# In-projection tiles in four parts, with the background steps between them

## What is computed

```python
proj = h @ w_in                       # 1024 -> 4608 columns
rq, rk, rv, rg, dq, dk, dv = jnp.split(proj, EVEN_SPLITS, axis=-1)
rq = rope(rq.reshape(B, L, H_RET, DK_RET), pos)
rk = rope(rk.reshape(B, L, H_RET, DK_RET), pos)
ro, s_fin = retention(rq, rk, rv.reshape(B, L, H_RET, DV_RET), s0)
ro = head_group_norm(ro).reshape(B, L, RET_V) * jax.nn.silu(rg.astype(F32))
dq = rope(rms_norm(dq.reshape(B, L, 2 * H_DIFF, DH_DIFF), qg), pos)
dk = rope(rms_norm(dk.reshape(B, L, 2 * H_DIFF, DH_DIFF), kg), pos)
k_all = jnp.concatenate([k_past, dk], axis=1)     # samples: 32 pages of 128 positions each
do = diff_attn(dq, k_all, v_all, pos, k_pos, lam)
mix = jnp.concatenate([ro, do], axis=-1) @ w_out
```

## Time and profile before

| | us |
|---|---|
| median of 3 runs | 2005.0 (2004.58 to 2010.87) |
| profiled execution | 2001.99 |
| its span | 2000.2 |
| TensorE busy | 1858.2 (93%) |
| VectorE, GpSimd, ScalarE busy | 897.7, 648.7, 603.4 |
| mean granted TensorE clock | 0.961 |

### The profile page before, as it was taken

The page is one execution under the profiler, slowest core; times in us unless marked ns, Lnnn a source line. Parts: engine busy times, 40 slices in busy tenths (PEclk is TensorE's granted clock), DMA queues, the critical chain, the costliest instruction groups (busy, mean ns, idle before and its releaser), DMA issues.

```text
span 2000.2 us, 31022 instructions
## 1 busy us (share of the span) xinstructions
PE 1858.2 (93%) x12203; PEld 1498.2 (75%) x12203; DVE 897.7 (45%) x1230; ACT 603.4 (30%) x986; POOL 648.7 (32%) x482
## 2 busy tenths in 40 slices
PE   4968888798889999999999999999999999999998
PEld 3866656566567777777778887767668799999997
DVE  3676554554667765543243325432223453223321
ACT  5323335433223231122233332131322332212311
POOL 0674323343456998634111000130221334103400
PEclk8888889899889999999999999999999999999999
DMA  7244534676878888865355565868783233323231
GB/s 251 91 143 127 169 127 158 198 253 224 293 263 274 267 286 295 304 190 176 125 170 147 190 201 177 284 207 284 254 281 106 86 95 94 95 88 93 84 103 57
DMA packets 296722, 365.43 MB, mean 183 GB/s; under 512 B 15625, under 2 KB 228186, under 8 KB 296330
## 3 DMA queue, kind: packets, MB, share of 16 engines
q1 hardware_dynamic: 289354, 355.36, 54.7%
q10 hardware_dynamic: 6640, 6.95, 1.0%
q0 software_dynamic: 592, 1.25, 0.5%
HBM read 352.29 MB, written 11.21 MB: 182 GB/s over the span
## 4 chain that ended last, share of the span: by engine, by line
PE 61%; issue 25%; DVE 5%; ACT 4%; POOL 3%; DMA 1%; SPq 1%; ACTq 0%; DVEq 0%; POOLq 0%
PE ps L2222 8%; PE ps L2224 8%; PE ps L2223 8%; PE ps L2309 6%; PE ps L2311 6%; PE ps L2310 6%; PE ps L2011 3%; PE ps L1945 3%; PE ps L1946 3%; PE ps L1947 3%; POOL tmp L938 2%; PE ps L2124 1%; PE ps L1917 1%; POOL g_lo L899 1%; DMA xst<-in_x_prompt 1%
## 5 line engine op out<-in xcount | busy, mean ns | idle before, releaser
L668 DVE TENSOR_TENSOR w_lo<-raw,w_hi 128x1024 fp32r<-128x1024 f32 x237 | 342.3, 1449 | 455.4 <-ACT w_hi L661 455.1
L879 POOL TENSOR_TENSOR kbuf<-kbuf,Qb 128x512 f32<-128x512 f32 x256 | 364.8, 1452 | 350.9 <-DMA kbuf<-in_cache_k 302.7
L661 ACT ACTIVATE w_hi<-raw 128x1024 fp32r<-128x1024 f32 x246 | 258.3, 1055 | 441.9 <-PE ps L2224 214.1
L1945 PE MATMUL ps<-w_hi,xg_hi 128*128 128x256 f32 x576 | 182.3, 317 | 5.1 <-ACT stg L1071 5.1
L2222 PE MATMUL ps<-xb_hi,w_hi 128*128 128x512 f32 x448 | 181.5, 405 | 0.0
L2224 PE MATMUL ps<-xb_hi,w_lo 128*128 128x512 f32 x448 | 177.1, 395 | 0.0
L938 POOL TENSOR_TENSOR tmp<-tmp,vn 128x512 f32<-128x512 f32 x24 | 32.4, 1371 | 445.6 <-ACT tmp L1320 445.6
L2223 PE MATMUL ps<-xb_lo,w_hi 128*128 128x512 f32 x448 | 176.5, 394 | 0.0
L1946 PE MATMUL ps<-w_lo,xg_hi 128*128 128x256 f32 x576 | 174.0, 302 | 0.0
L1947 PE MATMUL ps<-w_hi,xg_lo 128*128 128x256 f32 x576 | 173.0, 300 | 0.0
L1547 DVE TENSOR_REDUCE Sc<-kbuf 128x8 f32<-128x512 f32 x256 | 162.9, 675 | 21.8 <-POOL kbuf L879 21.7
(11 more groups left out here) (369 smaller groups left out, 3843.4 us busy)
## 6 DMA issues: line engine op xcount, KB each, us to landing
kbuf<-in_cache_k SPq DMA_DIRECT2D x256, 256.0 KB, 3.8
vbuf<-in_cache_v SPq DMA_DIRECT2D x256, 256.0 KB, 4.6
raw<-in_w_ffn_up SPq DMA_DIRECT2D x64, 512.0 KB, 4.0
raw<-in_w_ffn_down SPq DMA_DIRECT2D x64, 512.0 KB, 3.5
raw<-in_w_in_odd SPq DMA_DIRECT2D x48, 512.0 KB, 5.5
ring<-in_w_in_odd SPq DMA_DIRECT2D x48, 512.0 KB, 5.1
raw<-in_w_in_even SPq DMA_DIRECT2D x34, 512.0 KB, 4.9
ring<-in_w_ffn_up SPq DMA_DIRECT2D x32, 512.0 KB, 5.2
```

Of the source, the lines that this page charges most:

```text
L661: act.activation(w_hi[:, c.slot], source(c), ACT.Copy).then_inc(hi_made, 1)
L668: dve.tensor_tensor(w_lo[:, c.slot], source(c), w_hi[:, c.slot].bitcast(F32), ALU.subtract).then_inc(lo_made, 1)
L879: pool.tensor_tensor(kk, kk, Qb[:, s % 2, :], ALU.mult).then_inc(k_weighed, 1)
L1945: pe.matmul(out, xh, wh, start=kk == 0, stop=False, skip_group_check=True)
```

## The change

A slot now has four parts, and a tile's 24 matmuls are four groups of six: TensorE runs part 0, 1 and 2 of the slot's steps after the first, second and third group, and part 3 after the tile. The other engines run parts 0 to 2 ahead of the tile's evacuation or weight half and part 3 behind it. `plan()` places steps by quarters of a slot; steps that share one PSUM bank are kept two quarters apart (`apart`). The attention's 16 units start every 5.25 quarters (before every 4/3 slots, nearly the same), and within one the transpose stands 5 quarters and the product 7 quarters behind the scores. VectorE's half of `dE` is a step of its own, `dM`, and the rotary step `rot` is three. Page steps start at slot 12 instead of 4, at 1.5 ticks a tile (before 0.5 up to slot 17, then 1), 0.5 a slot in the tail (before 1), and 0.9, 0.9 and 1.0 beside the wide matrices (before 1.2, 1.2 and 1.3). `LO_SWITCH` 4 moves two weight halves from GpSimd to VectorE.

```diff
-FIRST_STEP = 4
+FIRST_STEP = 12
-LO_SWITCH = 5
+LO_SWITCH = 4
...
+    parts = [[[] for _ in range(4)] for _ in range(slots)]
+    def put(step, at):
+        parts[at // 4][at % 4].append(step)
+    def apart(step, bank, at):
+        while any(abs(at - t) < 2 for t in taken[bank]):
+            at += 1
+        taken[bank].append(at)
+        put(step, at)
...
-    for i in range(len(UNITS)):
-        j = read_of(3) + 6 + 4 * i // 3
-        middle[j].append(("dA", i))
-        early[j + 1].append(("dE", i))
-        first[j + 2].insert(0, ("dT", i))
-        late[j + 2].append(("dB", i))
+    first = 4 * (read_of(3) + 6)
+    for i in range(len(UNITS)):
+        at = first + 21 * i // 4
+        put(("dA", i), at)
+        put(("dE", i), at + 2)
+        put(("dM", i), at + 3)
+        apart(("dT", i), "turn", at + 5)
+        apart(("dB", i), "out", at + 7)
...
+        for n in range(NT):
+            put(("rA", h, n), at + 4 * n)
+            put(("rB", h, n), at + 4 * n + 2)
+        put(("rS", h), at + 17)
...
+        due = min(int(pace), len(ticks))
+        pace -= due
+        for n in range(due):
+            parts[j][3 if n == due - 1 else 1].extend(ticks.pop(0))
...
-PACE = {"rope": 0.5, "in": 1.0, "oe": 1.2, "up": 1.2, "dn": 1.3, "v": 1.0, "gate": 3.0, "u": 3.4}
+PACE = {"in": 1.5, "tail": 0.5, "oe": 0.9, "up": 0.9, "dn": 1.0, "v": 1.0, "gate": 3.0, "u": 3.4}
...
+                        if between is not None and kk % 2 and kk < KD - 1:
+                            between(kk // 2)
...
-                background(j)
+                                lambda q: run(PARTS[j][q:q + 1]))
+                else:
+                    run(PARTS[j][:3])
+                run(PARTS[j][3:])
```

More of the change, by code:

```diff
@@ L150, in plan @@
-    for m in ROPED:
-        first[read_of(m)].append(("rope" if m < 4 else "rot", m))
+    parts = [[[] for _ in range(4)] for _ in range(slots)]
+    taken = {"turn": [], "out": []}
+    def put(step, at):
[5 more added lines that the diff above has]
+        put(step, at)
+    for m in range(N_IN):
+        apart(("sT", m), "out", 4 * sample_at(m) + 5)
@@ L152, in plan @@
+    for m in ROPED:
+        at = 4 * read_of(m)
+        if m < 4:
+            put(("rope", m), at)
+        else:
+            for part in range(3):
+                put(("rot", m, part), at + 2 * part)
         for hh in range(2):
-            first[read_of(m) + 4 + hh].append(("turn", m, hh))
+            apart(("turn", m, hh), "turn", at + 14 + 3 * hh)
         if m > 5:
-            first[AT[m - 1, 2]].append(("rotS", m))
-    for i in range(len(UNITS)):
-        j = read_of(3) + 6 + 4 * i // 3
-        middle[j].append(("dA", i))
-        early[j + 1].append(("dE", i))
-        first[j + 2].insert(0, ("dT", i))
-        late[j + 2].append(("dB", i))
@@ L172, in plan @@
         for n in range(NT):
[L173 to L177, removed]
-        for p in range(NS // 2):
[L179 to L185, removed]
@@ L186, in plan @@
-    first[NTILE].append(("xB",))
+            put(("rC", h, n), at + (18 + n if last else 20 + 4 * n))
+        at = 4 * (read_of(10) + 6 + 6 * h)
+        put(("sL", h), at)
+        put(("sM", h), at)
+        for p in range(NS // 2):
+            put(("sU", h, p), at + 5 + 4 * p)
+        put(("sO", h), at + 21)
+    put(("so1",), 4 * (NTILE + 2) + 2)
+    put(("so2",), 4 * (NTILE + 4))
+    put(("soT",), 4 * (NTILE + 6))
+    for i in range(12):
+        put(("mix", i), 4 * NTILE + (2 * i if i < 6 else 2 * i + 2))
@@ L187, in plan @@
+    put(("xB",), 4 * NTILE)
     ticks = list(SAMPLE)
-    pace, after = 0.0, []
+    pace = 0.0
     for j in range(slots):
-        kind = ("rope" if j < read_of(3) else "in") if j < NTILE + TAIL else SLOT_KIND[j - NTILE - TAIL]
+        kind = ("in" if j < NTILE else "tail") if j < NTILE + TAIL else SLOT_KIND[j - NTILE - TAIL]
         if j >= FIRST_STEP:
             pace += PACE[kind]
[L193 to L201, removed]
+        due = min(int(pace), len(ticks))
+        pace -= due
+        for n in range(due):
+            parts[j][3 if n == due - 1 else 1].extend(ticks.pop(0))
@@ L1268, in _ @@
                 m, t = TILES[j] if j < NTILE else (N_IN, 0)
-                for step in AFTER[j]:
-                    if step[0] == "dE":
+                for part in PARTS[j][:3]:
+                    for step in part:
                         act_step(step)
@@ L1761, in _ @@
                 m, t = TILES[j] if j < NTILE else (N_IN, 0)
+                for part in PARTS[j][:3]:
+                    for step in part:
+                        dve_step(step)
                 if LO_SWITCH <= m < N_IN and t == 0:
@@ L1765, in _ @@
                     lo(dve, Chunk(0, 0, 0, 2 * m + AHEAD))
-                background(j)
+                for step in PARTS[j][3]:
+                    dve_step(step)
                 if LO_SWITCH <= m < N_IN and t == NT - 1:
```

84 lines of the change are left out of this document (44 added, 40 removed).

## The result

The change made the kernel slower by a little, 0.8%, but clear of the spread: 2016.43 us (median of 17 runs, 2011.34 to 2024.53) against 2003.24 (17 runs, 1994.52 to 2010.87), ratio 1.0076 with a 95% interval of [1.0061, 1.0091]. Forecast were 1937 and faster. The profiled execution took 2022.19 us, its span 2020.4.

What follows compares the result with a forecast made beforehand. Before the wide matrices TensorE lost 154 of 527 us to idle time and half clock; in them TensorE was the bound. With transfers setting tiles 27 to 73, -39 - 10 - 6 - 13 = -68 gave 1937 us, range 1895 to 1980.

Steps and rivals of the forecast that it cites:

- the 23 us of loss: Tiles 27 to 73: TensorE's idle and half-clock loss expected to remain after three quarters of 91.5 us went.
- 91.5 us lost: Tiles 27 to 73 before the change: TensorE's 52.2 us idle plus 39.3 us lost to the half clock.
- 14.6 us of TensorE's work: Tiles 27 to 73: fifteen more groups of four value pages at 0.97 us each, from 1.5 ticks a tile.
- the long stretch: Tiles 27 to 73, 166 to 523 us before the change: forecast to shrink from 357 to 318 us, -39.
- 280.5 forecast: Tiles 27 to 73: TensorE's work at full clock without waits, 265.5 us before plus the added value pages.
- the 318 us: Tiles 27 to 73: length forecast with transfers setting it, 92.9 MB at near 285 GB/s, against TensorE's 303 us.
- First stretch: -10 forecast: Tiles up to 26, 38 to 166 us before: 10 us saved (0 to 20) of 40 lost, VectorE over 80% busy.
- Tail and wide matrices: -6 and -13 forecast: Tail: two fewer value-page groups, 2 us, plus 4 of loss back; wide matrices: thirteen fewer groups at 0.97 us.
- The third: Rival: SP's single queue holds loads back, TensorE waits; tiles 27 to 73 take 392 us, total 2025; chance 0.14.
- The second: Rival: spreading hides little, other engines late by over a quarter; tiles 27 to 73 take 342 us, total 1975; chance 0.18.
- A range of its own from 1915 to 1965: Whole kernel: the main forecast's own range, long stretch at 300 or 326 us, first and tail at their ends; chance 0.53.

Runs made afterwards that it cites:

- e8: The change with before's page-step pace, and an attention unit's transposes and product two quarters later (slack); 1973.12 us, ratio 0.9859.
- e9: The change at its own fast pace, with an attention unit's transposes and product two quarters later (slack); 1999.78 us, ratio 0.9985.
- e14: e9 with SP issuing a slot's value loads ahead of its key loads; 1996.06 us, ratio 0.9975.
- e3: The change with TensorE running all four parts of a slot's steps behind the whole, unbroken tile; 2018.35 us, ratio 1.0089.
- e11: e8 with TensorE running all four parts of a slot's steps behind the whole, unbroken tile; 1975.31 us, ratio 0.9861.
- e7: The change with VectorE's page sums over 16 of the 64 columns of a key (short sums); 1993.84 us, ratio 0.9974.
- e16: e9 with VectorE's page sums over 16 of the 64 columns of a key (short sums); 1980.99 us, ratio 0.9892.
- e13: e9 with before's pace up to slot 26 and 1.5 page steps a tile only from slot 27; 1995.95 us, ratio 0.9956.
- e4: The change with the four rotary steps of the prompt's attention in part 3 instead of part 0; 2021.26 us, ratio 1.0097.
- e12: e8 with 0.87 page steps a tile instead of 1.0, and 1.3, 1.3 and 1.4 beside the wide matrices; 1950.7 us, ratio 0.974.
- e15: e8 with 0.75 page steps a tile, and 1.4, 1.4 and 1.5 beside the wide matrices; 1956.76 us, ratio 0.9764.
- e10: The change with SP issuing a slot's value loads ahead of its key loads; 2015.44 us, ratio 1.0073.
- e1: The change with before's page-step pace, its four parts and the places of all other steps kept; 2005.66 us, ratio 1.0017.

## Why the prediction was wrong

**The step that failed** is "A unit's scores, exponentials and transpose are now 5 quarters of a slot apart, and a bank's users two. ... So waits of this kind should mostly vanish", and the 23 us of loss that I left for the stretch. I compared a quarter with the wait that was there (3.9 us on `aT`), and not with the distance that the change took away. Before, two whole tiles stood between a unit's scores and its transposes; now it is five quarters instead of eight, of which two lie behind `dM`. Of 91.5 us lost, three quarters should have gone; 81.5 stayed. e8 and e9 show this step: two more quarters are worth 32 us at the old pace and 17 at the new. I had named VectorE's lateness as a rival and dismissed it because "waits of 2 to 4 us are what two quarters cover"; the wait in the timeline is made of 2.47 us idle and a 2.17 us weight half, and no page sum had to be late for it. VectorE's busy time itself came out as I had worked it out, 235.6 us against 231; in that wait its order made it late, not its load.

**The second step that failed** is the price of the pace, since the first is not the whole miss of 79 us by the medians. I had put 1.5 ticks a tile at 14.6 us of TensorE's work in the long stretch and at a gain of 10 in the first. With slack they cost 39 and 23 us (e9 against e8), and only 30 of these 62 come back in the tail and the wide matrices. I priced a page step by its own time on TensorE and by the transfers' rate, and not by what it holds up behind it.

**TensorE's work, 280.5 forecast, 303 measured.** My sum was off by itself: 265.5 and 14.6 are 280.1, and 265.5 should have been 270 by the table. Two terms make the rest, less 4 us at the other steps. The tiles' matmuls cost 15 us more where steps break them (155 against 139.5), which I had put at nothing. And 120 more value records cost 24 us instead of 14.6, in part because they waited for loads, as e14 shows. Neither is worth much by itself: e3 and e11 get the 15 us back and pay them at the other steps or as idle time, e14 gets 9 to 11 us of value records back for 4 in all.

**The transfers.** Bytes were right: 245 GB/s x 384.8 us = 94.3 MB, forecast 92.9. The rate was not the limit, as a DMA share of 0.74, e9's 253 GB/s, e7's 260 and e16's 264 show. So the 318 us never came into play. What held the stretch at 385 us is more than one thing: slack takes 12 us off it (e9), short sums 22 (e7), both together 27 (e16).

**First stretch: -10 forecast, +19.7 measured.** The weight load was no longer a wait of 9.9 us in one go, but two of 9.9 in all. I counted VectorE's page sums as work that fits, over 80% busy; it was busy for 107.0 of 147.7 us, 72%, and late all the same. ScalarE waits for its rotary steps:

```profile
100.62 0.22 ACT L1129 ACTIVATE tiny<-tiny 128x16 f32<-128x16 f32 x1 [10.74 <-DVE tiny L1476]
```

Everything that TensorE needs from ScalarE stands behind that row, `qT` and `sraw` first. With the old pace early and slack (e13) the stretch is 118.7 us, as in e8. Between e9 and e13, which differ here by the early pace alone, TensorE's waits fall from 9.8 to 1.7 us for weight loads and from 19.4 to 11.7 for `sraw`. e4 shows that moving the step does not help. The page sums themselves are a small part of the delay. Before L1476, for which ScalarE waits in that row, VectorE had done a rotary step and the samples' step, up to 94.3 us, and then only this of page sums:

```profile
94.28 3.63 DVE L1562 TENSOR_REDUCE Sc<-kbuf 128x8 f32<-128x512 f32 x6
```

Short sums take 3 us off the stretch in e7 and 8 in e16, of some 20. What makes the rest of the early pace's cost stays open.

**Tail and wide matrices: -6 and -13 forecast, -10.8 and -16.3 measured.** The size, in the wide matrices: beside the 104 value records fewer there are 16 matmuls on `osb` and four on `sqs` fewer, some 4 us, which I had left out. Why the tail gained more than 6 us stays open. The mechanism (TensorE is the bound in the wide matrices) stands: e12 and e15 pay for more pages with 12 and 24 us.

**The rivals.** The third gave the right sign and nearly the time, 2025, and put the turn at 372 us or 250 GB/s; measured were 385 and 245. But its mechanism, TensorE waiting for loads behind SP, was not the cause in the long stretch: e10 took the value pages' waits away and left the time. So the near hit is mostly luck. In the first stretch there is something of it: the 9.9 us for weight loads, which were there before as well, and which the old pace brings down to 4.1 (e1) and 1.7 (e8). The second had the mechanism (VectorE late by more than a quarter) and the wrong size and sign, since it had no cost for the shorter chain.

**The range.** "A range of its own from 1915 to 1965" does not follow from its terms: the long stretch at 300 or 326 with first stretch and tail at their ends gives 1905 and 1960. Neither holds the result.

**What the pace costs by itself.** With slack, 1.5 instead of 1.0 costs 27 us. By the stages of the two profiled executions: +23.4 first stretch, +39.1 long, -12.1 tail, -17.5 wide, which is 33 (the spans differ by 31). 31.6 of the 39.1 lie at the value records, half clock included: 52.8 us for 280, 188 ns each, instead of 21.2 for 160, 132 ns each. e14 shows that these can be had 9 us cheaper for a gain of 4. How the rest of the 27 divides between VectorE's load and the loads' order stays open.

## What to carry to other kernels

When steps are spread in finer parts, count for every producer and consumer the parts that lie between them before and after, and set them against the slowest single thing that may stand in the producer's queue with its own wait, here a weight half of 4.6 us against two quarters of 3. Here the finer order gained only with that distance kept: at before's pace it was worth 0 or 30 us by two numbers. Move background work toward the stage whose engine never waits and price it there, since that price is plain work (12 to 17 us here), while beside a chain of short steps the same work cost more in waits and clock than its own time. Stop where the two cancel, as between e12 and e15.

## What the hardware showed that I had not expected

Breaking a row of equal matmuls has a price on TensorE beside the step that is put in. At full clock, with no wait, in the profile of the change:

```profile
231.43 0.28 PE L1967 MATMUL ps<-w_hi,xg_lo 128*128 128x256 f32 x1
231.55 0.61 PE L2162 MATMUL ps<-dvn,aT 128*128 128x128 f32 x4
231.91 0.36 PE L1965 MATMUL ps<-w_hi,xg_hi 128*128 128x256 f32 x1
232.12 0.28 PE L1966 MATMUL ps<-w_lo,xg_hi 128*128 128x256 f32 x1
232.23 0.28 PE L1967 MATMUL ps<-w_hi,xg_lo 128*128 128x256 f32 x1
```

The first matmul behind the break is followed after 0.21 us, the others after 0.12. Over the whole long stretch, where the clock is full and nothing waits, the medians are 0.22 us for 107 first ones and 0.118 for 787 others; the kernel before has the same two values, for 32 and 859. So each break costs some 0.1 us beside the time of the step itself. The change has 122 groups of tile matmuls that follow a step, before has 45, so 77 x 0.105 makes an estimated 8 of the 15 us that the tiles' matmuls took more. Some 5 more lie at the last matmul ahead of a step, after which the next start comes 0.18 us later. With unbroken tiles the other steps took 12 us more (e11), which fits a price of changing from one kind of matmul to another, wherever that is; no run has it alone.

A weight half on VectorE takes a median of 1.619 us in 606 to 850 us of the change, where GpSimd is busy 58% of the time, against 1.826 at 80% in the earlier trace rows and 1.218 at 1% in the earlier trace rows; e8 has 1.757 at 74%. The price moves with GpSimd's load.

```profile
L680 DVE TENSOR_TENSOR w_lo<-raw,w_hi x39: 1206/1619/2366, 611.1 to 844.4; 128x1024 fp32r<-128x1024 f32 x39
```
